# First layer of a three-block kernel: where the weighted sum over attention groups is stored, loaded and placed

## The reference, cut to what matters

```python
def dilated_mixer(h, w_in, w_out):
    proj = h @ w_in
    ...                                   # q, k with rope, v, gate
    for g, (window, dil) in enumerate(DIL_GROUPS):
        o, lse = dilated_window_attention(q[g], k[g], v[g], window, dil)
        outs.append(o); lses.append(lse)
    alpha = jax.nn.softmax(jnp.stack(lses, axis=0), axis=0)
    o = jnp.sum(alpha[..., None] * jnp.stack(outs, axis=0), axis=0)
    y = o.reshape(B, S, DIL_WIDTH).astype(h.dtype) * jax.nn.silu(gate)
    return y @ w_out
```

## Time and profile before

| | us |
|---|---|
| median of three runs | 2536.58 |
| the three runs | 2529.98, 2537.23, 2536.58 |
| the profiled execution | 2531.03 |
| its span, from the first to the last instruction | 2529.1 |
| PE busy in the span | 2195.6 (87%) |

### The profile page before, as it was taken

One profiled execution on the slowest core, in us unless ns is written; L12 is line 12 of the kernel. 1 busy time (PEld: TensorE's weight loads), 2 busy tenths in 40 slices (PEclk: granted clock), 3 DMA queues, 4 the chain that ended last, 5 costly groups with the idle time before them and its releaser, 6 DMA issues. The chain is left out here.

```text
span 2529.1 us, 25974 instructions
## 1 busy us (share of the span) xinstructions
PE 2195.6 (87%) x10048; PEld 1736.3 (69%) x10048; DVE 961.0 (38%) x1587; ACT 862.4 (34%) x1660; POOL 904.9 (36%) x506
## 2 busy tenths in 40 slices
PE   4999999999736998856999999897987998999998
PEld 3877788888625876535677877676765546887876
DVE  1333335534262156662244231138453652110111
ACT  2454445654313455333232122232322222221231
POOL 3323233334433422143254434343224323443442
PEclk9999999999857999978999999998998998999999
DMA  4312122223331321122343333233123332332321
GB/s 158 92 50 77 52 75 83 81 87 85 116 145 50 95 67 52 66 79 62 100 139 112 100 76 100 63 99 93 53 90 122 126 103 83 100 93 90 99 93 59
DMA packets 132425, 225.50 MB, mean 89 GB/s; under 512 B 9512, under 2 KB 59224, under 8 KB 132096
## 3 DMA queue, kind: packets, MB, share of 16 engines
q1 hardware_dynamic: 110720, 168.63, 22.0%
q0 software_dynamic: 10896, 36.86, 4.5%
q10 hardware_dynamic: 10688, 18.35, 2.0%
HBM read 201.50 MB, written 21.71 MB: 88 GB/s over the span
## 5 line engine op out<-in xcount | busy, mean ns | idle before, releaser
L2170 POOL TENSOR_TENSOR lo_ring<-raw_ring,hi_ring 128x1024 fp32r<-128x1024 f32 (+1 forms) x304 | 731.3, 2427 | 1175.8 <-ACT hi_ring L1833 1175.6
L833 PE MATMUL bank<-xh,hi_ring 128*128 128x512 f32 x1472 | 599.5, 407 | 5.3 <-DVE xl L1306 3.2
L833 PE MATMUL bank<-xh,lo_ring 128*128 128x512 f32 x1472 | 581.0, 395 | 0.0
L833 PE MATMUL bank<-xl,hi_ring 128*128 128x512 f32 x1472 | 580.1, 394 | 0.0
L1833 ACT CAST hi_ring<-raw_ring 128x1024 fp32r<-128x1024 f32 (+1 forms) x304 | 303.4, 1046 | 508.6 <-PE bank L833 488.3
L833 PEld LDWEIGHTS bank<-xh,hi_ring 128*128 128x128 f32 x1472 | 281.4, 191 | 76.4 <-issue 18.1
L833 PEld LDWEIGHTS bank<-xh,lo_ring 128*128 128x128 f32 x1472 | 280.4, 190 | 61.3
L833 PEld LDWEIGHTS bank<-xl,hi_ring 128*128 128x128 f32 x1472 | 281.3, 191 | 57.7 <-issue 2.6
L833 PE MATMUL bank<-hi_ring,xh 128*128 128x512 f32 (+1 forms) x608 | 250.6, 412 | 11.3 <-POOL lo_ring L2170 6.3
L833 PE MATMUL bank<-hi_ring,xl 128*128 128x512 f32 (+1 forms) x608 | 242.4, 399 | 0.0
L833 PE MATMUL bank<-lo_ring,xh 128*128 128x512 f32 (+1 forms) x608 | 242.2, 398 | 0.0
(11 more groups left out here) (242 smaller groups left out, 2514.1 us busy)
## 6 DMA issues: line engine op xcount, KB each, us to landing
raw_ring<-in_ffn_w_in SPq DMA_DIRECT2D x176, 256.0 KB, 3.1
raw_ring<-in_dil_w_in SPq DMA_DIRECT2D x80, 512.0 KB, 3.6
raw_ring<-in_ffn_w_out SPq DMA_DIRECT2D x44, 512.0 KB, 3.7
raw_ring<-in_diff_w_in SPq DMA_DIRECT2D x32, 512.0 KB, 3.7
raw_ring<-in_w_in SPq DMA_DIRECT2D x32, 512.0 KB, 3.7
arena<-scratch_heads POOLq DMA_DIRECT2D x4, 1584.0 KB, 7.1
scratch_gates<-arena ACTq DMA_DIRECT2D x24, 256.0 KB, 2.1
arena<-scratch_gates POOLq DMA_DIRECT2D x24, 256.0 KB, 4.1
```

The lines of the kernel that those rows point to most:

```text
L833: ins = T.matmul(bank[b][:, 0:S if p.form == "feature" else p.cols], lhsT, rhs, start=(k == 0 and m == 0), stop=(k == p.K - 1 and m == len ...
L2170: G.tensor_tensor(lo, raw_ring[:, p % RAW, 0:q.kq * q.n], hi.bitcast(F32), ALU.subtract).then_inc(lowered, 1)
```

## The change

The planner's ratio at the gate panels goes from 1.6 to 1.9, so that unit 5's attention is written earlier among their products, and a new side stream `first_sum` stands behind it. The barrier ahead of the weighted sum is left out. The sum is cut into jobs, `mix_load`, `mix_ratio`, `mix_weight`, `mix_sum` and `mix`, and each tile's ratio, weights and sum are written one tile ahead of its `mix`, which is now the gate's multiplication and the transposes alone:

```diff
-UNIT_RATIO, GATE_RATIO = 0.85, 1.6
+UNIT_RATIO, GATE_RATIO = 0.85, 1.9
...
-    interleave(gate_panels(plan, w, 9 * D, 0), side, GATE_RATIO)
-    plan.job("over", True)
-    for n in range(NT + 1):
-        if n < NT:
-            plan.tile_parts("mix", n)
-        if n:
-            plan.job("lower", n - 1)
+    def first_sum():
+        plan.job("mix_load")
+        plan.job("mix_ratio", 0)
+        for _ in range(3):
+            yield
+        plan.job("mix_weight", 0)
+        plan.job("mix_sum", 0)
+        yield
+
+    interleave(gate_panels(plan, w, 9 * D, 0), chain(side, first_sum()), GATE_RATIO)
+    for n in range(NT):
+        if n + 1 < NT:
+            plan.job("mix_ratio", n + 1)
+        plan.tile_parts("mix", n)
+        if n + 1 < NT:
+            plan.job("mix_weight", n + 1)
+            plan.job("mix_sum", n + 1)
+        plan.job("lower", n)
```

All four tiles' heads have a buffer of their own in the arena, and the weights' small buffers are doubled. The gate of the first layer stays in the arena (`tile_gate`): its tanh and silu are made in place, and it is neither stored nor loaded; DVE's multiplication waits for the second gate panel instead. The third group moves from one POOL instruction to 16 ACT instructions, one for each head:

```diff
-                    H = heads[:, b].rearrange("p g (h r) -> p g h r", h=DIL_HEADS)
-                    G.wait_ge(weights_made, n + 1)
-                    w = corr[:, 32:48].unsqueeze(2).to_broadcast([P, DIL_HEADS, HD])
-                    G.tensor_tensor(H[:, 2, :, 0:HD], H[:, 2, :, 0:HD], w, ALU.mult).then_inc(third_weighed, 1)
...
+                elif kind == "mix_sum":
+                    n = a[0]
+                    A.wait_ge(weights_made, n + 1)
+                    for h in range(DIL_HEADS):
+                        o_ = heads[:, n, 2, h * ROW:h * ROW + HD]
+                        ins = A.activation(o_, o_, ACT.Copy, scale=corr[n % 2][:, 32 + h:33 + h])
+                    ins.then_inc(third_weighed, 1)
```

POOL stores a unit's heads in one transfer (units 0 to 3) or four (units 4 and 5), and loads all four tiles in one go as soon as all stores have landed:

```diff
-                for i in range(NT):
-                    if DIL[g] == 16:
-                        for rr in range(4):
-                            G.dma_start(rows_[4 * i + rr, :, hf * 8 * ROW:(hf + 1) * 8 * ROW],
-                                        st[32 * rr:32 * rr + 32, i].rearrange("p a b -> p (a b)")).then_inc(stored[buf], 16)
...
+                if DIL[g] == 16:
+                    for rr in range(4):
+                        G.dma_start(rows_.rearrange("(i r) l c -> r l i c", r=4)[rr], st[32 * rr:32 * rr + 32]).then_inc(stored[buf], 16)
+                elif DIL[g] == 4:
+                    G.dma_start(rows_.rearrange("i p c -> p i c"), st).then_inc(stored[buf], 16)
+                else:
+                    G.dma_start(rows_[0].rearrange("(i p) c -> p i c", p=P), st).then_inc(stored[buf], 16)
...
+                elif kind == "mix_load":
+                    for buf in range(2):
+                        G.wait_ge(stored[buf], 16 * (1 + 1 + 4))
+                    for n in range(NT):
+                        G.dma_start(heads[:, n], scratch[:, n * P:(n + 1) * P, :].rearrange("g p c -> p g c")).then_inc(heads_landed[n], 16)
```

More of the change, by code:

```diff
@@ L653, in program @@
         stage = carve(at, 2, NT, 8, ROW)
-        at = [0]
-        heads = carve(at, 2, 3, DIL_HEADS * ROW)
-        mix, mix_gate = carve(at, 2, D), carve(at, 2, D)
-        mins, corr, dens = small[:, 16:32], small[:, 32:80], small[:, 80:128]
+        mix_gate = [arena[:, a:a + D] for a in (0, D, 4 * S * 2, 4 * S * 2 + D)]
+        at = [4 * S]
+        mix = carve(at, 2, D)
+        at = [2 * 2 * 4 * S]
+        heads = carve(at, NT, 3, DIL_HEADS * ROW)
+        mins, corr, dens = [[small[:, a + b:a + c] for a in (16, 256)] for b, c in ((0, 16), (16, 64), (64, 112))]
         at = [0]
@@ L735, in program @@
         d_scored, d_exped = sem("d_scored"), sem("d_exped")
-        heads_landed = [sem(f"heads_landed{i}") for i in range(2)]
-        mix_gate_landed = [sem(f"mix_gate_landed{i}") for i in range(2)]
+        heads_landed = [sem(f"heads_landed{i}") for i in range(NT)]
+        gate_panel = {p.at: p for p in panels if p.kind == "gate"}
         corr_made, corr_exped, weights_made, third_weighed, heads_mixed, mixed = (
@@ L1238, in consume @@
                 m = 4 * p.n + o
-                if p.kind == "gate":
+                if p.kind == "gate" and p.at[0] == 0:
+                    g = tile_gate(o, p.at[1])
+                    V.wait_ge(gate_tanhed, m + 1)
+                    V.scalar_tensor_tensor(g, g, 1.0, psum, ALU.add, ALU.mult).then_inc(drained[o], 1)
+                elif p.kind == "gate":
                     b = o % 2
@@ L1376, in mix_tile @@
                 V.tensor_tensor(m, m, H[:, 2, :, 0:HD], ALU.add).then_inc(heads_mixed, 1)
+            def mix_tile(n):
                 V.wait_ge(heads_mixed, n + 1)
[L1378 to L1379 removed]
+                V.wait_ge(drained[n], gate_panel[0, 1].use[n])
+                V.scalar_tensor_tensor(mix[:, n % 2, :], mix[:, n % 2, :], 0.5, mix_gate[n], ALU.mult, ALU.mult).then_inc(mixed, 1)
             def lambda_():
@@ L2211, in gpsimd_program @@
                     p = panels[steps[s].panel]
-                    if steps[s].last and p.kind == "gate":
+                    if steps[s].last and p.kind == "gate" and p.at[0] == 1:
                         layer, c = p.at
```

90 lines of the change are left out of this document (44 added, 46 removed).

## The result

The changed kernel took 2520.52 us in the median of seven runs (2516.27 to 2525.74), the kernel before 2534.25 us in seven runs beside them (2529.98 to 2538.96). The ratio is 0.9944, with a 95% interval of 0.9928 to 0.9960: faster by 13.7 us. 2517 was predicted. The profiled execution took 2516.27 us with a span of 2514.5, against 2531.03 and 2529.1 before: 14.8 us less, where the prediction had 17.

A forecast was written before the change was run, and what follows sets the result against it. PE's wait for DVE's gate multiplication, in the 66.4 us between last gate product and first w_out product, bounds it. 13.6 at tile 0 plus 3.3 in three rounds, say 17 us, from 2533.7 gives 2517; range 2514 to 2526, chance 0.70.

The forecast's parts named there:

- the gate products: PE's products ahead of the mixed tiles: stay without a gap beside the denser attention, end near 680 as before; nothing charged.
- rival (c): Gate products: the tighter mix of attention and products stalls PE, 8 us; saving 9, 2525; chance 0.05.
- The landing: Load of tile 0's heads behind POOL's four stores: lands at 679.0, where it was 698.2.
- POOL's waking up: Ahead of POOL's first load: if 3 us belong to this instead of the barrier, the heads land at 682.
- Loads in the order of issue: The four head loads are served one after another, 3.9 us each, the further ones at 682.9, 686.8, 690.7.
- Rival (b): Head loads: all four share the DMA engines and land together at 690.7; saving 5.3, 2528; chance 0.09.
- Tile 0 behind the landing: Work from tile 0's load to the end of its gate multiplication: ends at 694.5 instead of 708.1, 13.6 us saved.
- The clash with POOL's `lo_ring`: DVE's multiplications in tile 0's sum, slowed by POOL's work on two w_out pieces: 1.1 us of a possible 3.4.
- The 16 copies: ACT's scaled copies of the third group, in each tile: 0.235 us each, 3.8 us for 16.
- (a): ACT's scaled copies overlap as plain ones do, 0.105 us each; saving 22.4, 2511; chance 0.12.
- (d): ACT's scaled copies cost 0.689 us each, 11.0 instead of 3.8 for 16; slower, 2545.5; chance 0.04.
- The round: From one tile's gate multiplication to the next: 10.85 us against 11.9; three rounds save 3.3.

## Why the prediction was right, step by step

**What bounds the kernel, the gate products.** PE is busy 49.15 of 50 us, the rest being what lies behind their end at 679.15 (679.8 before). No head cost PE a wait; rival (c) is out at a ratio of 1.9. Its price, however, is real at 2.6 and 3.2, where the products end 2.7 and 3.6 us late. There the prediction's way of pricing it, the wait alone, falls short: a wait of 1.2 us came to 2.7 with the lower clock behind it.

**The landing: 680.5 instead of 679.0.** The stores were issued from 666.2 on, 0.8 us earlier than predicted (0.65 of it by the earlier gate products), and the first landed in 2.9 us, the median of the earlier trace rows, but the fourth took 4.8: that median was too small for four transfers of 264 KB in flight together. (The prediction's own 668.6 + 2.9 is 671.5 and not 671.7.) The load behind it took 7.3 us, as in the earlier trace rows. The choice between "barrier" and "POOL's waking up" for the 3 us was right in its result, since the load was issued 0.5 us behind the landing (667.8 + 4.8 = 672.6 against 673.15) and not 3 us. But its name was only half right: the barrier by itself is 0.7 us, and the rest came with a gate store that was issued just ahead of it.

**Loads in the order of issue.** The four landings, 7.3 us after the first issue up to 18.4 after the fourth, are at 680.4, 684.3, 688.3 and 693.9; with the first landing's 1.4 us added, 684.3, 688.2 and 692.1 were forecast. The fourth is 1.8 us late, beside two pieces of w_out issued from 684.6 on; no engine waited for it. Rival (b), all at 690.7, is out.

**Tile 0 behind the landing: 15.2 us instead of 15.5.** The clash with POOL's `lo_ring` is there, with a size of 1.7 instead of 1.1 and at another place. The multiplications took 1.22 us each; what waited were two operations of 48 elements a partition ahead of them, L1383 (0.45 instead of 0.25) and L1389 (1.71 instead of 0.21), the latter to the end of POOL's second piece at 686.9. With the ratio of 1.6, where POOL is idle at that place, they took 0.24 and 0.21. By the Trainium skill ("SBUF — State Buffer", section "Who interferes with whom") the engine that issues first holds the shared ports for its whole instruction, whatever the shape of the other; the trace agrees, with 0.21 us of work held for 1.5 us. The 3.4 us that the same rule would have given needed both multiplications beside POOL. Tile 0's L1409 ends at 695.6 instead of 694.5, 12.5 us saved of 13.6. Only 11.8 of them lie in the stage, 16.5 us behind the last gate product instead of 28.3; the other 0.65 are the gate products' earlier end, which is the difference of two executions and no work of the change.

**The 16 copies: 3.93 us instead of 3.8.** Each lasts 0.335 us, the high end, and they start 0.24 apart, so that the step "0.335 less an overlap of 0.1" holds in both parts. Rivals (a) and (d) are out.

**The round: 10.55 instead of 10.85.** In its own steps: xh rounded at 2.63 (2.65), copies done and second addition at 6.57 (6.55), the rest 3.98 instead of 4.3: I had summed durations of DVE operations, and most of these, waiting for nothing, start 0.1 us ahead of their forerunner's end. In the last round no ratio stands, 10.13. Three rounds saved 4.6 us instead of 3.3. In the stage this stands against 1.8 us missing at tile 0, so that 16.4 of the forecast 16.9 are there; that two errors nearly cancel is luck in the sum.

**The tail** is 2.3 as before, and the first w_out product stands at 729.15 where 729 was forecast; so near a hit needed the 0.65 us too.

**The sum.** 17 us at that product, 14.6 at the end of the span, 13.7 between the medians. What has no term in the prediction is the 600 us ahead of the stage and the 1800 behind it, in which two executions of one kernel part by up to 6.5 us. The range 2514 to 2526 is wider than that, and the measured 2520.5 lies in its middle; that the median came within 4 us of 2517 says little on any single term, and the stage's own times say more.

## What to carry to other kernels

Where engines walk through one list of jobs, the gain of an earlier transfer is decided by what the list puts ahead of it on the issuing engine: a `lo_ring` pair ahead of the stores cost nothing at a ratio of 1.6, where it ended just as the last head was copied, and 4.4 us at 2.6, where it began just then. Move work to a free engine only together with its place in the order: the third group on ACT won nothing until its copies were written ahead of the gate multiplication, and then a round fell from 10.55 to 8.9 us. When attention is mixed more densely into the products, price a wait of PE at up to twice its length and more: 1.2 us of idle time came to 2.7 at one place, through the lower clock behind it, and to no more than itself at another. Compare such stages from their own start, since the rest of the program moves the whole by more than a small change does.

## What the runs showed of the hardware that I had not expected

- A barrier with a drain on POOL right behind an issued transfer held the queue 3.4 us, though the program didn't wait for the landing (2.3 us after issue); in the kernel before and in the same with a ratio of 1.9, which wait for the landing too, it was 5.47 us. With no transfer of POOL's in flight the barrier and its drain took 0.7 us. Where the 2.1 us between 3.4 and 5.47 come from was not tried.
- A DVE operation of 0.21 us took 1.71 us where it met an instruction of POOL that had begun before, and ended with it; where POOL was idle it took 0.21.
- PE waited 1.19 us amid full work, and behind it the granted clock was 0.50 for some 3 us; a wait of the same length at 607 us left it at 1.00. What decides between the two wasn't tried.
- Four stores of 264 KB issued 0.5 us apart landed 2.9 to 4.8 us after their issue, in order, and 4.8 to 6.2 with the ratios 1.6 and 2.6, where a piece of w_out was being loaded beside them; 16 small ones of 66 KB landed in 1.9 to 2.0 us each.
- Two executions of the changed kernel differ by 6.5 us with the same stage of 50 us; in the window 1160 to 1260 us the granted clock is 0.81 in one and 0.86 in the other.
